# Expert layers: more dots ahead of the spread, one-hot columns on three engines, and an earlier row search

## The reference

```
q = xt @ w_q                                   # 8 heads, two halves of 128
s = einsum('thcd,hcnd->thcn', q, keys)         # 128 scores a head and half
sv, si = top_k(s, 16)
cand = sv[:, :, 0, :, None] + sv[:, :, 1, None, :]
best, bi = top_k(cand, 16)                     # 16 of 256 sums a head
i1, i2 = si[.., bi // 16], si[.., bi % 16]     # expert i1 * 128 + i2
gate = softmax(best)
act = gelu(x . u_tab[e]) * gate                # 128 experts a token
out = sum_e act * v_tab[e]
```

## Time and profile before

| | |
|---|---|
| median of 3 runs | 4903.82 us (4902.18 to 4907.68) |
| the profiled execution | 4903.42 us |
| its span | 4901.7 us |
| TensorE (PE) busy | 4372.1 us, 89% |
| VectorE (DVE) busy | 2938.2 us, 60% |
| GpSimd (POOL) busy | 1630.8 us, 33% |
| ScalarE (ACT) busy | 799.3 us, 16% |
| mean granted TensorE clock | 0.945 of full speed |

### The profile page before, as it was taken

The page is one execution under the profiler, slowest core; times in us unless marked ns, Lnnn a source line. Parts: engine busy times, 40 slices in busy tenths (PEclk is TensorE's granted clock), DMA queues, the critical chain, the costliest instruction groups (busy, mean ns, idle before and its releaser), DMA issues. The chain is left out here.

```text
span 4901.7 us, 44839 instructions
## 1 busy us (share of the span) xinstructions
PE 4372.1 (89%) x15514; PEld 2539.6 (52%) x15514; DVE 2938.2 (60%) x5871; ACT 799.3 (16%) x1690; POOL 1630.8 (33%) x1568
## 2 busy tenths in 40 slices
PE   6799468977999999999969987698789999999997
PEld 2463344756455545554536865375655554555452
DVE  4444972888257476655674236379735756666477
ACT  1210441028100000000012223101820000000000
POOL 0000510019035464554530000001913655455464
PEclk8899779999999999999979988799999999999998
DMA  3120541116379899998951101211646998999896
GB/s 139 53 88 1 194 184 75 56 67 180 131 283 355 335 373 366 352 362 306 397 225 52 69 18 34 78 48 65 170 140 247 351 371 338 363 360 354 304 402 268
DMA packets 354147, 1048.49 MB, mean 214 GB/s; under 512 B 31641, under 2 KB 132361, under 8 KB 342234
## 3 DMA queue, kind: packets, MB, share of 16 engines
q0 software_dynamic: 148128, 545.35, 29.5%
q1 hardware_dynamic: 106748, 450.27, 24.4%
q10 hardware_dynamic: 99072, 50.33, 3.6%
HBM read 991.70 MB, written 54.14 MB: 213 GB/s over the span
## 5 line engine op out<-in xcount | busy, mean ns | idle before, releaser
L599 PE MATMUL banks<-blocks,dense_weight 128*128 128x512 f32 x3072 | 1382.0, 601 | 50.5 <-DVE dense_weight L774 50.3
L566 PE MATMUL banks<-h_dense_T,blocks 128*128 128x384 f32 x4096 | 1362.0, 487 | 37.7 <-DVEq L667 37.7
L566 PEld LDWEIGHTS banks<-h_dense_T,blocks 128*128 128x128 f32 x4096 | 779.2, 190 | 627.8 <-issue 109.6
L599 PEld LDWEIGHTS banks<-blocks,dense_weight 128*128 128x128 f32 x3072 | 591.1, 193 | 757.3 <-issue 699.0
L410 POOL DMA_INDIRECT expert_rows<-in_pk_u_dram,expert x512 | 646.0, 1262 | 800.8 <-DVE own_dots L789 355.6
L410 POOL DMA_INDIRECT expert_rows<-in_pk_v_dram,expert x512 | 598.6, 1169 | 496.5 <-DVE acc L808 209.6
L774 DVE TENSOR_TENSOR dense_weight<-dense_act,shared 128x384 f32<-128x384 f32 x256 | 218.3, 854 | 806.5 <-PE banks L599 742.9
L808 DVE SCALAR_TENSOR_TENSOR acc<-expert_rows,expert_weight,acc 128x1024 f32<-128x1024 f32 x504 | 624.1, 1284 | 63.8 <-DMA expert_rows<-in_pk_v_dram,expert 63.2
L789 DVE CUSTOM_DVE_ANT_0 expert_rows<-expert_rows,h_rows 128x1024 f32<-128x1024 f32 x512 | 595.0, 1220 | 0.1
L445 ACT ACTIVATE dense_act<-banks 128x384 f32<-128x384 f32 x256 | 125.7, 491 | 2358.6 <-PE banks L566 2332.6
L401 POOL TENSOR_SCALAR shared<-iota,picked_T 128x128 f32<-128x128 f32 x192 | 121.4, 648 | 521.8 <-ACT picked_T L451 460.4
(11 more groups left out here) (443 smaller groups left out, 4329.7 us busy)
## 6 DMA issues: line engine op xcount, KB each, us to landing
blocks<-in_pk_u_turned_dram SPq DMA_DIRECT2D x256, 512.0 KB, 6.1
blocks<-in_pk_v_dram SPq DMA_DIRECT2D x256, 512.0 KB, 6.8
gates_dram<-shared ACTq DMA_DIRECT2D x48, 1024.0 KB, 5.1
shared<-gates_dram SPq DMA_DIRECT2D x32, 1536.0 KB, 10.5
ada_block<-in_ada_rest_dram SPq DMA_DIRECT2D x32, 1280.0 KB, 7.7
blocks<-in_pk_w_q_dram SPq DMA_DIRECT2D x32, 512.0 KB, 3.3
MIXT<-in_ev_w_in_dram SPq DMA_DIRECT2D x16, 512.0 KB, 3.5
expert_rows<-in_pk_u_dram,expert POOLq DMA_INDIRECT x512, 7.8
```

What stands on the lines that cost most here:

```text
L566: mm = pe.matmul(dense_dots(c), u[:, k * P:(k + 1) * P], HT[:, k, :], start=(k == 0), stop=(k == KD - 1))
L599: mm = pe.matmul(ps[:, at_:at_ + HALF], wt[:, c % WEIGHED, z * P:(z + 1) * P], v[:, half_ * HALF:(half_ + 1) * HALF], start=(c == 0), stop ...
```

## The change

- AHEAD goes from 16 to 20, and EARLY becomes (0, 9, 13, 16): 9, 4 and 3 dots before the three `columns(z)`, and the first 16 dots go to banks 0 and 1 instead of 6 and 7. TensorE waits for the last scores to be read (`score_used`) only behind the first nine dots. ScalarE keeps its order: exponentials(z), the gelus of the lot, columns(z).
- The first-key columns follow the pattern HOT_MAKERS over 16 groups: 8 by GpSimd, 5 by ScalarE, 3 by VectorE, which does four tokens in one compare with broadcast operands.
- SyncE loads the first gate blocks at c = 1.
- VectorE does BEFORE = 33 steps of the row tiles' search before the first product, then 8 a chunk in chunks 0 to 2, then 3. FIRST_ROWS becomes 3.
- `dense_weight` and `best_part` lie in the memory of `picked_T` and `expert_weight`, which makes room for the larger ring. ScalarE's two exponentials for the row tiles come at c = 0 and 12.

```diff
-AHEAD = 16
+AHEAD = 20
-EARLY = 12
-SIDE = 3
-FIRST_ROWS = 16
+EARLY = (0, 9, 13, 16)
+BEFORE = 33
+FIRST_ROWS = 3
+HOT_MAKERS = "PAPDPAPADPAPPDAP"
+def maker(g):
+    return HOT_MAKERS[g % len(HOT_MAKERS)]
 def by_act(g):
-    return g % 8 in (1, 4, 6)
+    return maker(g) == "A"
+def side_steps(c):
+    return 8 if c < FIRST_ROWS else 3
...
-        wt = buf(ctx, nc, "dense_weight", [P, WEIGHED, DENSE])
+        wt = cols[:, :, :, :].rearrange("p z a t -> p (z a t)").rearrange(
+            "p (b t) -> p b t", t=DENSE)
+        at_part = act_w[:, :, :].bitcast(U32)
...
         def dense_dots(c):
-            return ps[:, (6 + c % 2) * HALF:(6 + c % 2) * HALF + DENSE]
+            bank = c % 2 if c < EARLY[ND] else 6 + c % 2
+            return ps[:, bank * HALF:bank * HALF + DENSE]
...
-                if c == BLOCKS // 2:
+                if c == 1:
...
-                    if by_act(n // 4):
+                    if maker(n // 4) != "P":
                         continue
...
             for z in range(ND):
                 exponentials(z)
-                for c in range(z * EARLY // ND, (z + 1) * EARLY // ND):
+                for c in range(EARLY[z], EARLY[z + 1]):
                     gelu(c)
                 columns(z)
...
-                if c in (11, 25):
-                    exponentials(3 if c == 11 else 4)
+                if c in (0, 12):
+                    exponentials(ND + c // 12)
...
-            pe.wait_ge(score_used, CODES)
             for z in range(ND):
-                for c in range(z * EARLY // ND, (z + 1) * EARLY // ND):
+                for c in range(EARLY[z], EARLY[z + 1]):
                     chunk_dots(c)
+                if z == 0:
+                    pe.wait_ge(score_used, CODES)
                 columns(z)
+            pe.wait_ge(dots_out, EARLY[ND])
...
+                    if n % 4 == 0 and maker(n // 4) == "D":
+                        dve.tensor_tensor(hot(first_hot, n, 4),
+                                          iota128[:, :].unsqueeze(1).to_broadcast([P, 4, P]),
+                                          cols[:, z, 0, t:t + 4].unsqueeze(2).to_broadcast(
+                                              [P, 4, P]), ALU.is_equal).then_inc(hot_by_dve, 1)
...
+            for _ in range(BEFORE):
+                next(last)
             for c in range(P):
                 weigh(c)
-                for _ in range(SIDE):
+                for _ in range(side_steps(c)):
                     next(last, None)
```

More of the change, by code:

```diff
@@ L232 @@
 BATCH = 16
-EARLY = 12
-SIDE = 3
-FIRST_ROWS = 16
+EARLY = (0, 9, 13, 16)
[4 more added lines that the diff above has]
+    return HOT_MAKERS[g % len(HOT_MAKERS)]
 def by_act(g):
-    return g % 8 in (1, 4, 6)
+    return maker(g) == "A"
 def before(g):
-    return sum(by_act(k) == by_act(g) for k in range(g))
+    return sum(maker(k) == maker(g) for k in range(g))
 def block_of_dots(c):
@@ L273, in experts @@
                "keys_in", "block_used", "q_out", "scored", "score_used", "exp_in", "exp_out",
-               "dve_line", "iota_done", "distances", "hot_by_act", "cols_set", "cols_turned", "cols_out", "hot_first",
+               "dve_line", "iota_done", "distances", "hot_by_act", "hot_by_dve", "cols_set", "cols_turned", "cols_out", "hot_first",
                "hot_second", "spread", "spread_out", "gates_put0", "gates_put1", "gates_got0",
@@ L278, in experts @@
             ctx, (rows_in, squared, ms_ready, rooted, h_ready, turned, ht_out, keys_in, block_used,
-                  q_out, scored, score_used, exp_in, exp_out, dve_line, iota_done, distances, hot_by_act, cols_set,
+                  q_out, scored, score_used, exp_in, exp_out, dve_line, iota_done, distances, hot_by_act, hot_by_dve, cols_set,
                   cols_turned, cols_out, hot_first, hot_second, spread, spread_out, gates_put0,
@@ L294, in experts @@
         at_of = buf(ctx, nc, "best_at", [P, ND, HEADS, TOPK], U32)
-        at_part = buf(ctx, nc, "best_part", [P, 2, SLOTS], U32)
         picked = buf(ctx, nc, "picked", [P, NT, 3, SLOTS])
@@ L372, in _ @@
                                      ).then_inc(gates_got[b], 16)
-                elif c % KEYS_A_GROUP == BLOCKS // 2 and c + KEYS_A_GROUP < P:
+                elif c > KEYS_A_GROUP and c % KEYS_A_GROUP == BLOCKS // 2 and c + KEYS_A_GROUP < P:
                     g = c // KEYS_A_GROUP + 1
@@ L507, in _ @@
                 spread_tile(z)
-            for c in range(EARLY, AHEAD):
+            for c in range(EARLY[ND], AHEAD):
                 gelu(c)
             for c in range(P - AHEAD):
-                if c in (11, 25):
-                    exponentials(3 if c == 11 else 4)
+                if c in (0, 12):
+                    exponentials(ND + c // 12)
                 gelu(c + AHEAD)
@@ L584, in spread_tile @@
                         pe.wait_ge(hot_by_act, before(g) + 1)
+                    elif maker(g) == "D":
+                        pe.wait_ge(hot_by_dve, before(g) + 1)
                     else:
@@ L719, in experts_of @@
                 line.settle()
-                line.count(dve.tensor_copy(at_f, at_part[:]))
+                line.count(dve.tensor_copy(at_f, at_part))
                 yield
```

## The result

The changed kernel takes 4830.1 us (median of 4 runs, 4826.6 to 4834.0) where the kernel before takes 4904.0: a ratio of 0.985, with a 95% interval of 0.983 to 0.987. The forecast was 4828, with a range of 4812 to 4856. The trace of the changed kernel has a span of 4824.8 us against 4901.7.

The account below looks back on a forecast made before the run. TensorE, busy 89% of the span, was taken as the bound, so only its waits and slow feeding could give time. Gains of 1 + 11.8 + 9.8 + 15.1 = 37.7 us a layer, 75.4 for two, gave 4828 us, range 4812 to 4856.

Parts of the forecast that it names:

- Place 1: TensorE's 18.9 us wait after the last score: early dots move it, not remove it; gain 1 us a layer.
- rival (d): The wait after the last score is filled after all, 18 us a layer: 4792 us; chance 0.04.
- the new wait on gelu(15): Before the spread: a new wait taking some 0.5 us off the gain from the early dots.
- Place 2: The one-hot columns in the 139.8 us spread: sharing them among three engines gains 11.8 us a layer.
- The price of sixteen groups: In the spread: sixteen groups of one-hot columns take 21.5 us instead of 23.46.
- VectorE's compare: In the spread: each new 128 x 512 compare takes 0.65 us and holds GpSimd at most about that long.
- Place 3: TensorE's 8.0 us wait before the first sum and its slow restart: earlier gate load gains 9.8 us a layer.
- rival (b): In the spread: VectorE's compare waits for a GpSimd column, 0.59 us each: 4839 us; chance 0.12.
- rival (c): First chunks: 33 steps, then eight, outlast TensorE's dots, so the first-sum gain vanishes: 4848 us; chance 0.10.
- Place 4: The 97.6 us tail of sums, slowed by VectorE's rows and their transfers: earlier rows gain 15.1 us a layer.

Follow-up runs that it names:

- Experiments 4: Changed kernel with its dots back in banks 6 and 7, all behind the wait for the last scores to be read: 4832.5 us.
- experiment 5: Changed kernel with ScalarE's gelus 0 to 4 put ahead of its first exponential: 4792.7 us.
- experiment 9: Changed kernel with each of VectorE's two-input four-token compares made as four one-input compares: 4830.8 us.
- experiment 1: Changed kernel with the old sharing of first-key columns, 10 groups in 16 by GpSimd, 6 by ScalarE, none by VectorE: 4848.7 us.
- Experiment 3: Changed kernel with the rows from chunk 16 on again, the early search steps kept: 4885.5 us.

## Why the prediction was right, step by step

- **Place 1**: the mechanism was read correctly, and the 1.0 us forecast is the 1.0 measured, but not for the stated reason. The wait is moved and keeps its length (18.9 to 18.4 us), because ScalarE's queue decides. Experiments 4 and 5 show it from both sides, and rival (d), 36 us more, is what experiment 5 gets with its reordered line. The early dots gave 0.1 us, though; the rest is the 0.8 us wait for the first columns, which the sum dropped without naming it, and the new wait on gelu(15) took 0.25 us, not 0.5.
- **Place 2** is the mis-sized term: 11.8 us a layer forecast, 4.5 and 8.9 measured. The price of sixteen groups was right, 21.65 us in layer 1 against 21.5. VectorE's compare was 0.60 us from its start to the next start (0.68 from start to end) instead of 0.65, and GpSimd's groups beside one grew from 2.33 to at most 2.99 us, as bounded. But experiment 9 has the same 21.6 us for sixteen groups without the two-input compare, so the size was right, but what sets it is not shown. Two things were missed. Six times the difference of the periods is not the difference of the spreads: the old one was 1 us shorter than six periods, the new one is 1 us longer. That the early search of Place 3 runs beside GpSimd's last group (experiment 1) was not seen, but costs the changed kernel only 0.3 us of this. And in layer 0 the faster groups ran into the transfers of the gates: a buffer was wanted again 5.4 us after it was sent off, and the transfers take 5.0 to 6.2. The prediction looked for what a faster spread would collide with among the engines only, and not among their buffers.
- The rule of the Trainium skill (SBUF — State Buffer, "SBUF: two separate sides") on the shared ports: on GpSimd's side these traces agree, its groups grew by up to 0.66 us beside a compare of 0.68, and by 2.2 us beside the sum of pairs of 2.28. The same section counts VectorE in a two-port performance mode among the holders. No trace tells the mode of an instruction; in the slower stretch of experiment 9 a GpSimd column grew by 0.06 us, from 0.60 to 0.66, far less than the 0.3 us of a whole VectorE column. That VectorE's compare waits for GpSimd, rival (b), no trace shows: it takes 0.68 us in 33 of 34 cases in the changed kernel's spreads, 0.76 once.
- **Place 3**: 10.5 us a layer against 9.8. Product 0 came at 1263.7, 13.5 us after the end of the spread and 4 us earlier than worked out: VectorE ended its columns 4.4 us ahead of TensorE, not 2, and the 33 steps took 18.0 us, not 19. Hence product 1 was in time as well, and rival (c) did not come up.
- **Place 4**: 15.0 against 15.1. Experiment 3 shows that it is the rows, and that AHEAD = 20 without them would have cost more than the old tail.
- What was not in the sum: 3.5 and 1.8 us in the loop. The hand-over waits are as long as before, but the sums behind them take 5.4 or 7.1 us where they took 8.3 and 7.6. That is about half of the 10.2 us that Place 2 lacked. Also 3 to 7 us between the layers. Part of that is visible: over this stage TensorE is busy 703.1 us before and 699.1 after with the same matmuls; at the start of layer 1's queries its granted clock is 0.63 and 0.72 in the first 7 to 10 us in the two traces before and 1.00 in both after, and VectorE waits 3.6 and 3.5 us for the row scales instead of 4.8 and 4.3. What brings this about is open, and no kernel was made to find out.

So the total was near partly by luck: of 75.4 us forecast, the four places gave 66.3. The chunk loop gave 5.3 more, the stage between the layers 7.1, and the stage ahead of layer 0's last score took 1.9 back. None of these was in the forecast.

## What to carry to other kernels

Before moving work into an idle stretch, read the queue of every engine that must free its buffers: here the matmuls could start, but not go on, until a gelu that stood behind an unrelated exponential. Do then what the traces ask for: two reordered places on ScalarE gave some 60 us, nearly as much as the whole change. And when a stage gets faster, list what is sized in its old pace, transfers out of a ring of two buffers as well as engines.

## What the runs showed of the hardware

- A two-input VectorE instruction of 2.28 us lengthened a GpSimd group of four one-input columns from 2.33 to 4.53 us (changed kernel) and 4.44 us (experiment 1), nearly by its own length; VectorE's took 2.28 us all the same.
- One-input instructions of 128 elements run beside each other at two paces: 0.60 us a column for GpSimd with 2.3 to 2.4 us for eight of VectorE's, or 0.66 with 2.7. Both occur in one spread of experiment 9, with VectorE busy all the time in both; what brings on the slower one is open.
- Some waits of about 2 us of TensorE within the spread were followed by a lowered granted clock (0.66 over 5 us, 16 records of a 128-column matmul in 3.44 us instead of 1.95), but one of 2.18 us in the same spread was not (1.00 over 5 us), nor were the regular waits of 1.2 to 1.5 us in layer 1.
- Landing times of the same transfer of 1 MB ranged from 5.0 to 6.2 us. That was enough to cost a stage that uses it every 5.4 us some 4 us.
